# Block attention of a two-layer transformer: values computed by rows of tokens for four heads at once, ahead of queries and keys

## What is computed

```python
def moba_mixer(h, w_qkv, w_o, cos_h, sin_h):
    qkv = (h @ w_qkv).reshape(bsz, s_len, 3, A_HEADS, A_HEAD_DIM)
    q = apply_rope(qkv[:, :, 0], cos_h, sin_h).transpose(0, 2, 1, 3)
    k = apply_rope(qkv[:, :, 1], cos_h, sin_h).transpose(0, 2, 1, 3)
    v = qkv[:, :, 2].transpose(0, 2, 1, 3)
    o = moba_attention(q, k, v)
    return o.transpose(0, 2, 1, 3).reshape(bsz, s_len, A_HEADS * A_HEAD_DIM) @ w_o
```

## Time and profile before

| | |
|---|---|
| median of the runs | 1863.51 us (1861.65 to 1863.53, 3 runs) |
| the profiled execution's own time | 1861.66 us |
| its span, first to last instruction | 1859.7 us |
| TensorE busy | 1842.6 us, 99% |
| VectorE busy | 1318.0 us, 71% |
| ScalarE busy | 914.3 us, 49% |
| GpSimd busy | 53.6 us, 3% |
| share of 16 DMA engines in the queue of loads | 33% |
| block attention, first unit to first matmul of the output projection behind the loop | 364.4 to 535.4 us |

### The profile page before, as it was taken

The page is one execution under the profiler, slowest core; times in us unless marked ns, Lnnn a source line. Parts: engine busy times, 40 slices in busy tenths (PEclk is TensorE's granted clock), DMA queues, the critical chain, the costliest instruction groups (busy, mean ns, idle before and its releaser), DMA issues.

```text
span 1859.7 us, 31170 instructions
## 1 busy us (share of the span) xinstructions
PE 1842.6 (99%) x12175; PEld 1693.9 (91%) x12175; DVE 1318.0 (71%) x1742; ACT 914.3 (49%) x1386; POOL 53.6 (3%) x51
## 2 busy tenths in 40 slices
PE   8999999999999999999999999999999999999999
PEld 7899988988889899998898999989988898999888
DVE  6888862487656888882288888822888488888623
ACT  6455552355545545562255555622666464455522
POOL 0000000011100000000000000000000000000000
PEclk9999999999999999999999999999999999999999
DMA  6244343232223333333323343333221232343331
GB/s 183 80 113 113 91 115 102 79 90 72 77 57 102 91 91 106 97 104 106 108 57 108 91 113 104 102 98 104 63 63 57 69 91 84 99 112 105 109 102 47
DMA packets 339464, 174.64 MB, mean 94 GB/s; under 512 B 11070, under 2 KB 337836, under 8 KB 339372
## 3 DMA queue, kind: packets, MB, share of 16 engines
q1 hardware_dynamic: 338656, 172.25, 33.0%
q10 hardware_dynamic: 716, 1.11, 0.2%
HBM read 171.24 MB, written 2.10 MB: 93 GB/s over the span
## 4 chain that ended last, share of the span: by engine, by line
PE 85%; DVE 9%; ACT 3%; issue 2%; DMA 0%; POOL 0%; DVEq 0%; SPq 0%; ACTq 0%
PE acc L1881 19%; PE acc L1882 19%; PE acc L1883 19%; PE duo L1881 9%; PE duo L1883 9%; PE duo L1882 9%; DVE wl L1175 2%; DVE xg L1220 1%; DVE mx L1534 1%; PE acc L2147 1%; DVE probT L1555 1%; ACT prob L889 1%; DVE y L1240 1%; ACT wh L641 0%; DVE xT L1247 0%
## 5 line engine op out<-in xcount | busy, mean ns | idle before, releaser
L1881 PE MATMUL acc<-xg,wh 128*128 128x256 f32 (+1 forms) x1040 | 340.4, 327 | 2.4 <-DVE xg L1220 1.0
L1883 PE MATMUL acc<-xg,wl 128*128 128x256 f32 (+1 forms) x1040 | 336.9, 324 | 0.0
L1882 PE MATMUL acc<-xg,wh 128*128 128x256 f32 (+1 forms) x1040 | 336.8, 324 | 0.0
L1175 DVE TENSOR_TENSOR wl<-raw,wh 128x1024 fp32r<-128x1024 f32 (+2 forms) x198 | 228.9, 1168 | 126.5 <-ACT wh L641 126.2
L1882 PE MATMUL acc<-hT,wh 128*128 128x512 f32 (+1 forms) x704 | 255.2, 363 | 0.0
L1881 PE MATMUL acc<-hT,wh 128*128 128x512 f32 (+1 forms) x704 | 255.2, 363 | 0.0
L1883 PE MATMUL acc<-hT,wl 128*128 128x512 f32 (+1 forms) x704 | 255.2, 362 | 0.0
L641 ACT ACTIVATE wh<-raw 128x1024 fp32r<-128x1024 f32 (+2 forms) x198 | 194.4, 1011 | 116.4 <-PE acc L1883 71.8
L1881 PEld LDWEIGHTS acc<-xg,wh 128*128 128x128 f32 x1040 | 197.7, 190 | 20.5 <-issue 3.1
L1883 PEld LDWEIGHTS acc<-xg,wl 128*128 128x128 f32 x1040 | 197.7, 190 | 15.8
L1882 PEld LDWEIGHTS acc<-xg,wh 128*128 128x128 f32 x1040 | 197.9, 190 | 14.9
(11 more groups left out here) (283 smaller groups left out, 4175.6 us busy)
## 6 DMA issues: line engine op xcount, KB each, us to landing
raw<-in_ffn_w_dram SPq DMA_DIRECT2D x238, 512.0 KB, 4.2
raw<-in_ffn_w_dram SPq DMA_DIRECT2D x32, 384.0 KB, 3.4
raw<-in_moba_w_qkv_dram SPq DMA_DIRECT2D x24, 512.0 KB, 3.8
raw<-in_moba_w_o_dram SPq DMA_DIRECT2D x8, 512.0 KB, 3.8
raw<-in_mla_w_o_dram SPq DMA_DIRECT2D x8, 512.0 KB, 3.7
xin<-in_x_dram SPq DMA_DIRECT2D x4, 512.0 KB, 5.4
raw<-in_mla_w_dq_dram SPq DMA_DIRECT2D x4, 512.0 KB, 3.9
raw<-in_mla_w_uq_dram SPq DMA_DIRECT2D x8, 256.0 KB, 2.9
```

What stands on the lines that cost most here:

```text
L1175: v.tensor_tensor(wl[:, slot, 0:tiles], raw[:, slot, 0:tiles], f32(wh[:, slot, 0:tiles]), ALU.subtract).then_inc(w_lo, 1)
L1881: t.matmul(dst, w_h, m_h, start=start, stop=False, skip_group_check=onto)
L1882: t.matmul(dst, w_h, m_l, start=False, stop=False, skip_group_check=onto)
L1883: return t.matmul(dst, w_l, m_h, start=False, stop=stop, skip_group_check=onto)
```

## The change

**Values.** All values come first. Their weights are loaded as blocks of two feature tiles by four heads (256 x 512, again 512 KB, `V_UNITS` = 8 units of the 24). In `values_product` the tokens are stationary (128 tokens of `xg`) and the weights move (512 columns: four heads of 128), so that the result has tokens on the partitions and no transpose is needed. `all_values` takes the place of `quad`: heads 0 to 3 over each half of the tokens, then heads 4 to 7. The norm's factor, now one number per partition, is multiplied in at the split (`values_hi` on ScalarE, `values_lo` on VectorE), which writes into the place where the outputs of the heads will lie.

**Queries and keys.** Both projections of a head follow each other, and the loop runs two heads ahead: in iteration h TensorE projects query and key of head h+2. The lists of ScalarE and VectorE are written anew for it, and so is the part of `out_proj` for this stage (`moba_heads`), which has two heads' scores left, not one.

The core of `all_values`:

```diff
+            def all_values(xg0, n_post, n_pre):
+                u, r = U0[1], R0[1]
+                pe.wait_ge(evacuated, r - LAST[n_post])
+                for e in range(2):
+                    for k in range(KD):
+                        if e == 0:
+                            pe.wait_ge(w_lo, u + k // 2 + 1)
+                        pe.wait_ge(xg_ready, xg0 + KD * e + k + 1)
+                        for c in range(HT * e, HT * (e + 1)):
+                            ins = values_product(att_banks[1][c], k // 2, k, c, k == 0, k == KD - 1)
...
+                        if (e, k) == (0, 0):
+                            post_mean(n_post, 1)
+                        if (e, k) == (0, 3):
+                            post_spread(n_post, 1)
+                        if (e, k) == (1, 4):
+                            mean(n_pre)
+                        if (e, k) == (1, 7):
+                            spread(n_pre)
```

TensorE's loop over the heads:

```diff
-            for h in range(HEADS - 1):
+            for h in range(2):
+                qk_unit(h, 0)
+                qk_unit(h, 1)
+            for h in range(HEADS - 2):
                 moba_scores(h)
                 if h:
                     prob_transposes(h - 1, (0, 1))
-                    qkv_unit(3 * h + 4)
+                qk_unit(h + 2, 0)
+                if h:
                     prob_transposes(h - 1, (2,))
-                    qkv_unit(3 * h + 5)
                     values(h - 1)
-                if h + 2 < HEADS:
-                    if h == 0:
-                        pe.wait_ge(v_lo, 1)
-                    qkv_unit(3 * h + 6)
-                if h + 2 < HEADS:
-                    value_transposes(h + 1, r + 3 * h + 6)
+                qk_unit(h + 2, 1)
```

VectorE's loop:

```diff
-            for h in range(1, HEADS - 1):
-                products(h + 1, 0)
+            for h in range(HEADS):
                 softmax_mask(h)
-                probT_split(h - 1, (0, 1))
+                if h:
+                    probT_split(h - 1, (0, 1))
                 softmax_max(h)
-                rotated(h + 1, 0)
-                split(u + 3 * h + 7)
-                if h == 1:
+                if h + 1 < HEADS:
+                    for i in range(2):
+                        rotated(h + 1, i)
+                softmax_norm(h)
+                if h:
                     probT_split(h - 1, (2,))
-                softmax_norm(h)
-                products(h + 1, 1)
-                if h > 1:
-                    probT_split(h - 1, (2,))
-                split(u + 3 * h + 8)
-                rotated(h + 1, 1)
-                o_split(h - 1)
-                split(u + 3 * h + 9)
-                evac_v(u + 3 * h + 6, att_banks[1][3 * h + 5][:])
-                v_split(h + 1)
+                for i in range(2):
+                    if h + 2 < HEADS:
+                        products(h + 2, i)
+                    if i and h:
+                        o_split(h - 1)
+                    if h + 1 < HEADS:
+                        split(u + 14 + 2 * h + i)
```

And TensorE behind the loop, up to the wait for the last exponentials:

```diff
+                def moba_heads():
+                    last_scores(last - 1)
+                    prob_transposes(last - 2, (0, 1))
+                    pe.wait_ge(evacuated, att - 1)
+                    pe.wait_ge(o_lo, last - 3)
+                    heads_done(0, 0, HEADS - 4)
+                    prob_transposes(last - 2, (2,))
+                    values(last - 2)
+                    pe.wait_ge(evacuated, att)
+                    heads_done(1, 0, HEADS - 4)
+                    last_scores(last)
+                    prob_transposes(last - 1, (0, 1))
+                    pe.wait_ge(o_lo, last - 1)
+                    heads_done(0, HEADS - 4, HEADS - 2)
+                    prob_transposes(last - 1, (2,))
+                    values(last - 1)
+                    heads_done(1, HEADS - 4, HEADS - 2)
```

More of the change, by code:

```diff
@@ L415, in values_of, with values_part @@
         def values_of(n):
+            if n < HEADS:
+                return tuple(oT[:, a, n].rearrange("p (t d) -> p t d", d=P) for a in range(2))
             return vh[:, n % 2, 0], vh[:, n % 2, 1]
+        def values_part(i, a):
+            g, c = divmod(i, TS)
+            return oT[:, a, VG * g:VG * (g + 1), c * P:(c + 1) * P]
         def o_of(n, a):
@@ L538, in _ @@
             qkv = kpn(moba_w_qkv[0])
-            plain(U0[1], qkv, [HEADS * P * a + P * h for h in range(HEADS) for a in range(3)])
+            for i in range(V_UNITS):
+                g, j = divmod(i, KD // 2)
+                slot_free(U0[1] + i)
+                sp.dma_start(raw[:, i % SLOTS].rearrange("p (k h) n -> p k (h n)", k=2),
+                             qkv[:, 2 * j:2 * j + 2, (2 * HEADS + VG * g) * P:(2 * HEADS + VG * (g + 1)) * P]
+                             ).then_inc(raw_full[i % SLOTS], 16)
+            plain(U0[1] + V_UNITS, qkv, [HEADS * P * a + P * h for h in range(HEADS) for a in range(2)])
             plain(U0[1] + 3 * HEADS, kpn(moba_w_o[0]), range(0, D, P))
@@ L973, in _, with values_hi @@
             x_update(X_F0, N_F0, gain(0, 1, 0), u, gain(0, 2, 0), N_PRE1)
[L974 to L978, removed]
+            def values_hi(i):
+                g, c = divmod(i, TS)
+                if c == TS - 1:
+                    act.wait_ge(unit_done, u + KD // 2 * (g + 1))
+                else:
+                    act.wait_ge(values_psum, (TS - 1) * g + c + 1)
+                act.wait_ge(rtok_ready, RT0[N_PRE1] + 1)
+                s.activation(values_part(i, 0), att_banks[1][i][:].rearrange("p (h d) -> p h d", d=P), COPY,
+                             scale=rtok[:, c:c + 1]).then_inc(v_hi, 1)
             def exchanged(h, i):
[L981 removed]
+                exchange(evacuated, r + V_RES + 2 * h + i + 1, (rope_q, rope_k)[i])
             def rotated(h, i):
@@ L987, in rotated @@
                 part((qh, kh)[i][:, 0], (rope_q, rope_k)[i][1][:])
+            split(u + 4)
+            split(u + 5)
+            load_table(EXP)
+            for i in range(TS):
+                values_hi(i)
+            for w in range(6, 11):
+                split(u + w)
             probT_zeros()
+            for i in range(TS, 2 * TS):
+                values_hi(i)
+            split(u + 11)
             for i in range(2):
@@ L1639, in _ @@
[L1639 to L1655, removed]
-                products(h + 1, 0)
+            for i in range(TS):
+                values_lo(i)
@@ L1657, in _ @@
+            for w in range(6, 11):
+                split(u + w)
+            for i in range(TS, 2 * TS):
+                values_lo(i)
+            split(u + 11)
+            for i in range(2):
+                products(0, i)
+            for i in range(2):
+                rotated(0, i)
+            for i in range(2):
+                split(u + 12 + i)
+                products(1, i)
+            for h in range(HEADS):
                 softmax_mask(h)
-                probT_split(h - 1, (0, 1))
+                if h:
+                    probT_split(h - 1, (0, 1))
@@ L1673, in _ @@
[L1673 to L1678, removed]
+                if h + 1 < HEADS:
+                    for i in range(2):
+                        rotated(h + 1, i)
+                softmax_norm(h)
+                if h:
+                    probT_split(h - 1, (2,))
+                for i in range(2):
+                    if h + 2 < HEADS:
+                        products(h + 2, i)
+                    if i and h:
+                        o_split(h - 1)
+                    if h + 1 < HEADS:
+                        split(u + 14 + 2 * h + i)
```

139 lines of the change are left out of this document (75 added, 64 removed).

## The result

The changed kernel takes 1905.34 us (median of 4 runs, 1904.02 to 1906.03), the kernel before 1863.47 beside it: 2.26% longer, ratio 1.0226, 95% interval 1.0209 to 1.0244. The forecast was 1891, the range 1875 to 1900. The direction was right, the size was not: +41.9 us where +28 was worked out. What the sum had at nothing, and should not have, is the clock of TensorE behind each wait.

A forecast was written before the change was run, and what follows sets the result against it. TensorE was taken as the bound, with a VectorE and ScalarE chain that just fits beside it. Savings, a wait for the squares and stalls summed to +28.1 us, giving a median of 1891 us, range 1875 to 1900.

The forecast's parts named there:

- the sum: Whole kernel: savings, wait for the squares and stalls of heads 1 to 7 added up to +28.1 us.
- TensorE is the bound and the chain beside it just fits: Attention loop before: TensorE 99% busy; the VectorE and ScalarE chain ends 0.06 us before its reader starts.
- the chain: Changed loop, end of key's projection to reader of last piece: 13.7 us, where TensorE arrives after 9.75.
- The waits: TensorE stalls for probabilities: 4.1 us in iteration 1, 3.9 each in 2 to 5, then 1.6, 5.1 and 5.3.
- the matmuls: Values stage: column count unchanged, 96 matmuls a group in 21.8 us, 0.228 us per 512 columns.
- the wait for the squares: TensorE asks for the mean of squares before VectorE ends it: a new wait of 0.5 to 1.1, taken 1.0 us.
- The savings of the rows: TensorE's list: 1.3 us from wider matmuls, 2.9 from dropped value transposes, 0.4 from a wait gone.
- The clock falls too: Rival: TensorE's clock drops behind stalls, up to 5.5 us each; two longest alone +11 us, 1902; chance 0.10.
- the main case: The forecast itself: the chain makes TensorE wait in every head, median 1891 us; chance 0.71.
- The cover: Rival: the chain does not bind, no stall in the values, -3.6 us, 1860; chance 0.07.
- the chain was no shorter than its rows: Judges the rival of more ScalarE and VectorE overlap, chain 2.7 us less, about +12 us, 1875; chance 0.10.
- The weighing of the 256-column matmuls: First stage, 192 matmuls of 256 columns become 96 of 512: 1.3 us saved by rows, 0.2 by the page's rule.

The follow-up runs named there:

- the old order: Seven useless VectorE operations ahead of the last piece of probabilities in heads 2 to 6, against the kernel before: 1890.83 us, ratio 1.0154.
- the two last runs: Changed kernel, values behind key's projection and side lists reordered: 1857.67 us; the same with the mean-of-squares transposes later and the factor's spread moved: 1857.08 us.
- Either order alone: Changed kernel with only the lists of ScalarE and VectorE reordered: 1877.99 us; with only values moved behind the key's projection on TensorE: 1884.74 us.

## Why the prediction was right and wrong

**Right: TensorE is the bound and the chain beside it just fits.** Everything that followed is the loss of that fit. One reading of it was wrong: the 0.06 us between the end of the last piece (468.68) and its reader (468.74) are no room. The same 0.06 lies there in the changed kernel, where TensorE stands waiting (482.40 and 0.61 for the piece, 483.07 for the reader), so it is the hand-over. In the kernel before, the values of the five heads in which VectorE waits for that piece take 2.03 to 2.07 us. Where it is there early, they take 1.92:

```profile
423.15 0.39 PE L1881 MATMUL duo<-probT,vh 128*128 128x512 f32 x1
...
425.07 0.40 PE L1881 MATMUL acc<-xg,wh 128*128 128x512 f32 x1
```

So TensorE already waited some 0.1 us a head for this chain, less than the view of waits shows.

**Right: the chain.** Worked out at 13.7 us from the end of the key's projection to the reader of the last piece, measured 13.78 (469.29 to 483.07); the mask worked out at 5.5, measured 5.62. The waits were worked out at 31.7 us (4.1, 15.6, 1.6, 5.1, 5.3), measured 31.1 in eight waits (4.5, four of 3.9, 1.8, 4.6, 4.7). The four in the loop are right to 0.02 us each; that the total is so close is in part luck, as 0.4 too little for the first and 0.5 and 0.6 too much for the last two partly cancel. The links of the chain, each read from a row of the kernel before, added up to within 0.1 us.

**Right: the matmuls.** 96 matmuls of the second group of values take 21.9 us (390.58 to 412.46); tokens as stationary operand and weights as moving one cost no more. The wait for the squares was taken as 1.0 and is 0.8. The savings of the rows are 4.6 us, 3.6 with the wait for the squares; the two last runs are 5.5 us (without that wait) and 4.9 (with it) below the kernel before. Two terms that the sum did not have go that way, by an estimate from the rows: some 0.1 us in each of five heads for the wait just named, and 0.08 us for each head's scores (the last section). The runs of the kernel before lie up to 1.9 us apart, so no more can be said of the rest.

**Wrong: "The clock falls too", chance 0.10.** That step failed. The sum put the clock at nothing. The prediction had the mechanism as a rival and bounded it at nothing to 5.5 us for each stall, but gave it one chance in ten, and priced two stalls of seven. The clock fell behind all seven waits for a last piece in the profile of this kernel (its mean is 0.99 in all four runs), and in the old order as well. By the trace the six matmuls of values behind each wait take 1.45 us, not 0.82, and the key's projection 6.4 or 7.5, not 5.5; over all seven, with the output matmuls behind the last two, that is 15 us, and filling the waits gave back 12.9. That is 1.8 to 2.2 us a fall, far below the upper bound. The argument against it, that no stall of that length is in the trace of before, was no evidence: a kernel without long waits can't show what they do. The page "TensorE: Matmul & The Clock Gate" of the Trainium skill, in the table "Why this matters for your kernels", warns that idle gaps between matmul bursts bring the clock back to half. Here the trace agrees, with 0.50 of the clock behind each such wait. Its rule should have carried the main case. By the trace, 31.1 us of waits and 0.8 for the squares, less 4.6 saved, are 27.3; with 15 for the clock that is 42, and 41.9 were measured.

**The other rivals.** The cover didn't hold (TensorE waits), and the chain was no shorter than its rows (13.78 us for 13.7). Both are true of the last two runs, with the values behind the key's projection and the side lists in another order. Either order alone, as tried here, left 16 and 23 us of loss.

**The weighing of the 256-column matmuls.** By the 2.5 ns beside the columns in the same page of the Trainium skill (section "Back-to-back issue gap") the front would have given 0.2 us, by the rows 1.3. The traces side with the rows: from the first matmul of the stage to the first of the second group it is 25.5 us before (364.41 to 389.89) and 24.9 after (365.72 to 390.58). Without the waits on record in these stretches (0.2 and 1.1) the gain is 1.5 us. A matmul of 512 columns takes 0.228 us after as before.

## What to carry to other kernels

Work taken out of the bounding engine's loop is also cover taken from the chains beside it: before, a head had 15.3 us between scores and the reader of the last piece, after, 9.75, and a chain that just fitted no longer did. Moving work ahead paid here only with the lists beside it put in order, so that nothing that waits for the newest result stands ahead of the oldest one's next step. When a wait of some 4 us between matmuls is forecast for TensorE, count about 2 us more behind it for the clock: in these runs the clock fell behind every such wait of 3.7 to 5.6 us and behind none of 1 to 2 us, and no wait between these lengths is on record. The 6 us ahead of the first matmul of the program are an exception that no run here explains: the profile gives a clock of 1.00 behind them.

## What was not expected of the hardware

- Matmuls whose results nobody reads, put into the waits, made the program some 13 us faster (12.9 against the runs beside each, 14.6 between the medians), as they kept the clock at 1.00.
- 12 matmuls of scores take 2.02 us behind float32 transposes and 1.93 us (469.29 to 471.22) behind matmuls. So behind the transposes of values the next matmuls lose some 0.08 us beside the 0.36 of the transposes, which the sum had not.
- 2 us of useless work on VectorE in each of five heads, straight ahead of the piece that bounds a head, cost no more than the runs can tell (1862.80 against 1862.55), because the chain there ran over ScalarE while VectorE idled. "Just fits" was true of the chain, not of each engine in it.
